# Two transformer blocks in fp32 on one core: gate logits in column groups, far rows, squares, expert order and fillers moved

## What is computed

```python
m = (silu_c @ ada_w[i] + ada_b[i])[:, None, :]            # adaptive vectors, sh1, sc1, g1, sh2, sc2, g2
o = dense_attention(q_rot, q, k, v, kc, vc)               # MLA heads, latent rows
y = o.reshape(B, S, H * DV) @ w_o                         # output projection
h_lat = layer_norm(DEEPNORM_ALPHA * h_lat + g1 * y, ln1_g[i], ln1_b[i])
f = conv_ffn(modulate(h_lat, sh2, sc2), ...)              # u = conv(h @ w_in); (silu(g) * a) @ w_out

# second block
gates = jax.nn.sigmoid(gate_logits.astype(f32)).reshape(b, s, G, R, 3)     # 24 columns of h @ w_in
o_hg = hgrn2_mixer(hg_q, hg_f, hg_i, lb)
o_hg = rmsnorm(o_hg, hg_norm[layer]) * jax.nn.silu(hg_g...)
for e in range(N_EXPERTS):                                # 32, d_ff 512
    hid = jax.nn.silu(t @ w_gate[e]) * (t @ w_up[e])
    out = out + combine[:, e:e + 1] * (hid @ w_down[e])
return rmsnorm(x, final_norm)
```

## Time and profile before

| | before |
|---|---|
| median of 3 runs | 1923.35 us (1923.25 to 1924.73) |
| the profiled execution | 1930.62 us, span 1928.9 us |
| mean granted PE clock | 0.966 |
| PE busy | 1761.5 us, 91% |
| weight loads of PE | 1363.9 us, 71% |
| DVE busy | 893.9 us, 46% |
| ACT busy | 362.7 us, 19% |
| DMA | 395.64 MB, 205 GB/s mean |

### The profile page before, as it was taken

How to read it: one execution, slowest core, us unless ns; L and a number is a source line. 1 busy time by engine, 2 the same in 40 slices (tenths; PEclk the granted TensorE clock), 3 DMA queues, 4 the chain that set the end, 5 groups by cost and what they waited for, 6 DMA issues and landing times.

```text
span 1928.9 us, 33169 instructions
## 1 busy us (share of the span) xinstructions
PE 1761.5 (91%) x14152; PEld 1363.9 (71%) x14152; DVE 893.9 (46%) x1909; ACT 362.7 (19%) x859; POOL 0.2 (0%) x4
## 2 busy tenths in 40 slices
PE   7999999999999999999999999999999766666666
PEld 4455546888888887777888888888788554555545
DVE  1488837766667327667554412478333211111112
ACT  0343403111110014222211102202321100000001
POOL 0000000000000000000000000000000000000000
PEclk9999999999999999999999999999999987888889
DMA  9534321222221207445344543323286999999996
GB/s 377 223 132 165 142 87 44 88 87 87 87 103 65 116 33 229 153 154 196 120 146 159 206 165 131 131 74 124 88 351 252 421 429 429 428 428 428 429 428 267
DMA packets 32508, 395.64 MB, mean 205 GB/s; under 512 B 3616, under 2 KB 6688, under 8 KB 8736
## 3 DMA queue, kind: packets, MB, share of 16 engines
q1 hardware_dynamic: 32416, 394.31, 51.2%
HBM read 393.25 MB, written 1.05 MB: 204 GB/s over the span
## 4 chain that ended last, share of the span: by engine, by line
PE 77%; DMA 19%; DVE 2%; ACT 1%; issue 1%; SPq 0%; DVEq 0%
PE bank L547 23%; DMA ring<-w_moe 17%; PE bank L1759 13%; PE bank L600 8%; PE bank L1487 6%; PE bank L3211 3%; PE bank L1972 3%; PE bank L843 2%; PE bank L1968 1%; PE bank L753 1%; PE bank L1145 1%; DMA ring<-w_ada 1%; PE bank L2328 1%; PE bank L1121 1%; PE bank L2024 1%
## 5 line engine op out<-in xcount | busy, mean ns | idle before, releaser
L547 PE MATMUL bank<-layer_input,ring 128*128 128x256 f32 x1152 | 257.4, 384 | 0.0
L547 PEld LDWEIGHTS bank<-layer_input,ring 128*128 128x128 f32 x1152 | 220.5, 193 | 33.1 <-issue 3.0
L3211 PE MATMUL bank<-ring,arena 128*32 128x128 f32 x1920 | 77.3, 326 | 54.6 <-DMA ring<-w_moe 52.1
L3328 DVE TENSOR_TENSOR arena<-arena,bank 128x128 f32<-128x128 f32 x32 | 9.2, 288 | 230.6 <-PE bank L3211 230.6
L1759 PE MATMUL bank<-arena 128*128 128x256 f32 x504 | 115.6, 379 | 0.0
L3211 PEld LDWEIGHTS bank<-ring,arena 128*32 128x32 f32 x1920 | 66.3, 131 | 66.5 <-DMA ring<-w_moe 61.8
L1487 PE MATMUL bank<-arena,ring 128*128 128x256 f32 x480 | 107.0, 380 | 2.4 <-ACT arena L1582 1.4
L1759 PEld LDWEIGHTS bank<-arena 128*128 128x128 f32 x504 | 95.8, 190 | 13.0
L1487 PEld LDWEIGHTS bank<-arena,ring 128*128 128x128 f32 x480 | 90.7, 190 | 16.5 <-ACT arena L1582 2.8
L600 PE MATMUL bank<-arena,ring 128*128 128x256 f32 x452 | 99.1, 380 | 0.9 <-DVE arena L2131 0.6
L3211 PE MATMUL bank<-arena 128*32 128x128 f32 x2008 | 70.2, 297 | 28.9 <-DMA arena<-w_moe 27.6
(11 more groups left out here) (484 smaller groups left out, 2708.7 us busy)
## 6 DMA issues: line engine op xcount, KB each, us to landing
arena<-w_moe SPq DMA_DIRECT2D x46, 2048.0 KB, 26.5
ring<-w_moe SPq DMA_DIRECT2D x45, 2048.0 KB, 25.9
ring<-w_ffn_in SPq DMA_DIRECT2D x22, 2048.0 KB, 8.0
ring<-w_ada_late SPq DMA_DIRECT2D x8, 3072.0 KB, 10.0
ring<-w_ffn_out SPq DMA_DIRECT2D x8, 2816.0 KB, 9.6
ring<-w_proj SPq DMA_DIRECT2D x7, 3072.0 KB, 10.2
ring<-w_na_pair SPq DMA_DIRECT2D x8, 1536.0 KB, 6.3
arena<-w_far SPq DMA_DIRECT2D x11, 1024.0 KB, 6.9
```

The costliest lines, as they stand in the source:

```text
L547: last = pe.matmul(out, a, b, start=(k == 0), stop=(k == len(lhs) - 1))
L3211: ins = eng.matmul(bank[x][group[q], 0:P], xe[:, k, SLOTS * e:SLOTS * e + SLOTS], weight(e, last, (x * KT + k) * FE + q * P, P), start=(k ...
```

## The change

Five things are moved. (1) In the last head pair, the adaptive chunk has five tiles (`ADA_LAST`, `ada_tiles`), which takes two products of rows from DVE; eight fillers stand ahead of the transposes and three behind the value product; DVE's first `mid` of every pair goes between the two rounds of maxima; the barrier at the end of the stage becomes two waits of PE. (2) In `out_split` the far rows' rest becomes a step of its own, `FAR_REST`, between products 6 and 7. (3) The gate logits are summed in four groups of 32 columns in `gate_sums`, DVE copies the groups, and two products with a constant (`fold24`) add them, behind the spread; three fillers instead of four. (4) ACT takes the recurrence's squares at head four. (5) The expert kept in spare memory is the third (2) instead of the 29th (28); the first quad is written out without a scatter and the two clears ahead of it go; in the last quad the scatter of experts 28 and 29 comes behind expert 30's gate, the held gate of expert 31 ahead of expert 30's down, experts 30 and 31 are scattered from tiles of their own in two turns of row groups (`scatter_alone`), and the last down matrix is loaded in two pieces.

```diff
@@ heads @@
+        if who == "pe":
+            b, taken, before = self.mla_turn(s, ("ada", ADA_LAST))
+            eng.wait_ge(taken, before + 1)
+            self.fill(eng, 3, b)
+            _, taken, before = self.mla_turn(s, ("av", MLA_PAIRS - 1))
+            eng.wait_ge(taken, before + 1)
         self.ada_rest(who, eng)
-        self.phase_end(eng, who)
...
-            half = 4 + u % 2
+            half = 6 if u == ADA_LAST else 4 + u % 2
...
             ada(u, 0)
+            if u == ADA_LAST:
+                b = claim(("av", u))
+                self.fill(pe, 8, b)
             turn(u)
...
             dve.tensor_scalar(nb[:, 0:4], mx[:, 0:4], -scale, None, ALU.mult).then_inc(s["max_ready"], 1)
+            mid(u, 0, 0)
             dve.wait_ge(s["scored"], 2 * u + 2)
...
-            mid(u, 0, 0)
             turned(u)
-            mid(u, 0, 1)
-            ada(u)
-            mid(u, 1, 0)
-            attended(u)
-            mid(u, 1, 1)
+            if u < ADA_LAST:
+                mid(u, 0, 1)
+                ada(u)
+                mid(u, 1, 0)
+                attended(u)
+                mid(u, 1, 1)
+            else:
+                ada(u)
+                mid(u, 0, 1)
+                attended(u)
@@ out_split @@
                 if i == 6:
                     eng.wait_ge(s["snapped"], OUT_SNAPPED[c, 4])
                     eng.wait_ge(s["sums_ready"], ready + (4 if c else 7))
+                    last = product(a, w21, t3, False)
+                if i == FAR_REST:
                     eng.wait_ge(s["up_used"], used_0 + c)
-                    rest(d, c, 1, CTX, start=True)
-                    last = product(a, w21, t3, False)
+                    last = rest(d, c, 1, CTX, start=True)
...
-                eng.wait_ge(s["up_done"], OUT_DONE[c, 6])
+                eng.wait_ge(s["up_done"], OUT_DONE[c, FAR_REST])
@@ mixer, PE @@
+            for k in range(KT):
+                j = 32 * (k % 4)
+                last = pe.matmul(bank[6][j:j + 32, 0:LAT], self.V[:, w + k * 24:w + k * 24 + 32], x[k], start=(k < 4),
+                                 stop=(k >= 4), skip_group_check=True)
+            last.then_inc(s["front_mm"], 1)
         def gate_logits():
+            pe.wait_ge(s["cmp_steps"], self.GATE_COPIED)
             for t in range(2):
-                last = self.mm(pe, bank[6][:, t * 24:(t + 1) * 24], [xk[:, t * P:(t + 1) * P] for xk in x],
-                               [self.vec("w_gate24", k * 24, 24) for k in range(KT)])
+                last = pe.matmul(bank[6][:, LAT + t * 24:LAT + (t + 1) * 24], sums[:, t * P:(t + 1) * P],
+                                 self.con("fold24"), start=True, stop=True)
             last.then_inc(s["front_mm"], 1)
...
         first_groups()
+        gate_sums()
+        spread()
         gate_logits()
-        spread()
-        self.fill(pe, 4)
+        self.fill(pe, 3)
@@ mixer, DVE @@
         dve.memset(v["blk"], 0.0).then_inc(s["cmp_steps"], 1)
+        dve.wait_ge(s["front_mm"], self.GATE_SUMS)
+        dve.tensor_copy(v["E0"][:, 0:LAT], bank[6][:, 0:LAT]).then_inc(s["cmp_steps"], 1)
@@ mixer, ACT @@
-            if u == 5:
+            if u == 4:
                 act.wait_ge(s["hg_mm"], self.HG_OUT)
@@ router @@
-        for n in ("gwt", "y"):
-            dve.memset(v[n], 0.0)
@@ experts @@
-RESIDENT = EXPERTS - QUAD
+RESIDENT = 2
...
+        sp.dma_start(self.expert_slots()[e][:, UPS:split], self.W["moe"][LAST][:, UPS:split])\
+            .then_inc(self.expert_loaded()[e][2], 16)
+        sp.dma_start(self.expert_slots()[e][:, split:], self.W["moe"][LAST][:, split:]).then_inc(self.sem("kept_in"), 16)
...
+        def scatter_alone(e, turn):
+            for t in range(2):
+                for h in ((turn + t) % 2, (turn + t) % 2 + 2):
+                    q = group[(h + e) % 4]
+                    ins = eng.matmul(bank[4 + 2 * t + h // 2][:, (h % 2) * 256:(h % 2) * 256 + 256], gwt[q, h, t, :],
+                                     alone[e][q, :], start=False, stop=(e == QUAD - 1), skip_group_check=True)
+                    if e == 2 or not turn:
+                        ins.then_inc(link, 1)
...
-                    if e == 0:
+                    if e == 0 and not first:
...
+                    if last and e == 2:
+                        eng.wait_ge(s["gwt_copied"], i * 2 + 2)
+                        eng.wait_ge(s["y_dve"], x + 1)
+                        eng.wait_ge(s["y_act"], x + 1)
+                        for t in range(2):
+                            scatter(t)
...
+                    if last and e == 2:
+                        eng.wait_ge(s["silu_done"], x + 1)
+                        project(0, QUAD - 1, last=True).then_inc(s["gate_done"], 1)
...
+                    if e == QUAD - 1 and last:
...
+                        scatter_alone(2, 0)
+                        eng.wait_ge(link, quads + 4)
+                        scatter_alone(2, 1)
...
-            with eng.Fori(0, quads - 1) as i:
+            quad(0, first=True)
+            with eng.Fori(1, quads - 1) as i:
                 quad(i)
-            quad(quads - 1, True)
+            quad(quads - 1, last=True)
             eng.wait_ge(s["y_dve"], EXPERTS + 1)
-            eng.wait_ge(s["y_act"], EXPERTS + 1)
-            for t in range(2):
-                scatter(t, stop=True).then_inc(self.sem("var_ready"), 1)
+            eng.wait_ge(link, quads + 8)
+            scatter_alone(3, 0)
+            eng.wait_ge(link, quads + 12)
+            scatter_alone(3, 1)
```

149 lines of the change are left out of this document (96 added, 53 removed).

## The result

The changed kernel takes 1911.36 us (median of 4 executions, 1909.52 to 1912.92) beside 1923.82 for the kernel before (4 executions); the ratio is 0.9934, 95% interval 0.9917 to 0.9952. That is 12.5 us, where 18.6 was forecast: it is faster, as forecast, but 6.7 us above the predicted time (1904.7) and 0.4 above the range. Over the whole study the changed kernel was taken three times (13 executions, median 1909.95) beside 72 executions of the kernel before on three chips (median 1924.94, 1922.8 to 1929.2), with ratios of 0.9934, 0.9921 (0.9904 to 0.9937) and 0.9922 (0.9908 to 0.9935). So the change is worth some 12.5 to 15 us; the median of all 13 lies inside the range, 5.2 us above the forecast.

The account below looks back on a forecast made before the run. Bound: TensorE until about 1490 us, then the experts' weight stream at 428 GB/s. Terms 4.3 + 1.9 + 2.4 + 5.0 + 5.0 = 18.6 us took the median to 1904.7; range 1899.5 to 1911.0.

Parts of the forecast that it names:

- The base: Differences read from the profiled execution, 1930.62 us, carried unscaled to the unprofiled median, 1923.35, which is 7.3 less.
- Squares: Recurrence, squares moved to head four: 1.6 us wait before head five's sum goes, and 3.4 of half speed; 5.0 us.
- Heads' end: Last head pair: output projection starts at about 241.8 instead of 244.40, 2.6 us, plus 1.7 of clock; 4.3 us.
- Transposes and the clock: Last head pair: 2.8 us of transposes might count as a gap for the clock, losing the 1.7 us.
- Far rows: First feed-forward's second product: 0.64 us wait on ScalarE goes in three of four output chunks; 1.9 us, between 1.0 and 2.0.
- Gate logits: Projection after the gates 2.0 us sooner, up to 1.9 more by the clock; 2.4 us taken, between 0 and 4.0.
- Experts: Expert stage: start, end and closing scatter, (a) to (c), with rounding for one stall; 5.0 us, between -1 and 8.
- (a): Start of the expert stage: without the first scatter, 3.72 us, the hole in the weight stream shrinks; 0.7 us.
- (b): End of the expert stage: PE keeps up with the stream, last weights land at 1909.6, last product ends at 1913.2.
- (c): Closing scatter in two turns: 1.5 us in all against 3.72, first half summed at 1914.9 against ScalarE's start at 1919.66.
- The first, the clock: Rival: the clock falls anyway in thin stretches left; 1.7 + 3.4 + 0.9 us lost, giving 1910.7; chance 0.13.
- the second rival: Experts' gain does not come: PE at 0.50 in last quad, scatter before expert 30's up; 5.0 lost, 1909.7; chance 0.18.

## Why the prediction was wrong

- **The base.** "I carry the sum of differences over to it unscaled" is the step that failed. The profiled execution stood 7.3 us above the median, and I named the number and asked no further. A second execution took 1923.98, and the excess lay in the very places that I priced: 3.3 us at head five, 1.6 at the gate logits, 1.8 in the experts. What an unusual execution loses can't be won back from the usual one. The term that it spoiled most is the next.
- **Squares, 5.0.** Mis-sized: 1.9 us (1.7 in the traces of usual executions). The wait of 1.6 was right. The half speed that I priced at 3.4 came in 2 of 6 executions, 3.3 us each time, and both were the slowest of their kernels; by that frequency it is worth about 1.1 in the mean and nothing in the median.
- **Heads' end, 4.3.** Right: 3.8 to 4.6 alone, 4.5 in the traces. The steps stand too: the projection at 241.5 (forecast 241.8), DVE's product out of the way, 1.7 us of clock (in the four of seven executions without the edit in which the projection's clock fell). Of the value product's start I had 238.2, and it was 237.87.
- **Transposes and the clock.** In the changed kernel 24 transposes behind fillers ran in 3.21 us at 1.00, and the projection began at 1.00; without the fillers they took 4.53 with the clock at 0.50, and the projection still began at 1.00. By the rule of the Trainium skill ("TensorE: Matmul & The Clock Gate", Part 4, PE-mode transpose) the 1.7 us would have stayed lost; in ten executions with this edit, nine of them with fillers, they never were.
- **Far rows, 1.9.** The traces show 2.2, the times 0.6 to 0.9 with an interval that holds both. The mechanism is seen, its size is not settled by the times.
- **Gate logits, 2.4.** Right in size: 1.5 to 1.7 alone, 2 to 4 within the whole. From the last product of the norm's sums to the sixtieth record of the projection the traces read 21.6 us in the mean of eight executions without the edit and 18.7 in nine with it. The new wait for the copy (forecast 0.6, measured 0.98) was foreseen. A fall of the clock and "the clock at 1.00" both occurred, in 3 and 6 of 9 executions.
- **Experts, 5.0.** Mis-sized: 3.9 in the traces, 2.5 to 2.9 alone by the times. (a) gives nothing: the hole in the stream stays, so the first scatter was not its cause, and the second one, which did go, brings the end of the stream no nearer. (b) and (c) together were to give 4.3 and gave 3.9, of which up to 2 may be the stall inside expert 31's up, which no step of the sum named. The closing scatter, from last down to the end, gave 1.3 (14.2 to 12.9), less than my step (c), since ScalarE had read the first half while PE was summing the second in the old kernel too. Two turns of one scatter take 1.6 us with their wait, as the row of the rope scores gave (1.5). But "here only two work together" was a misreading. Within a turn the four products use four different row groups, and 30 ns behind the first start four records are in work at once:

```profile
1897.32:1897.34 0.02, 0.02 (x4) 0.02 (x4) 0.00 (x0) 0.00 (x0) 0.00 (x0) 1.00 0.00 0
```

  The 3.07 times that the Trainium skill gives for four row groups ("TensorE: Matmul & The Clock Gate", Part 3, Measured speedup) would make it 1.2, by an estimate from that figure; here 3.72 against 1.6 is 2.3 times, with two turns and the 0.17 us of wait between them.
- **The rivals.** The first, the clock, came in another form than I gave it: not that falls stay in the changed kernel, but that they were not in the usual kernel before. (At the gate logits they do stay, in 3 of 9.) I had made it 1910.7 at a chance of 0.13; that this is close to what was measured is luck, since the terms that make it up are others. Half-speed work at expert 30's gate, part of the second rival, is real: 3.5 to 3.6 us instead of 1.95 in three of six executions with this end, and the stage 1.6 us longer in them. The stream did not starve.

With the terms at their measured sizes, 4.5 + 2.2 + 2.7 + 1.7 + 3.9 and 0.7 for the weights of the second product, the sum is 15.7. From the median of the 72 executions of before, 1924.94, that gives 1909.2, and 13 executions of the changed kernel gave 1909.95. The 12.5 of the first comparison is a small sample on both sides: before had 1923.82 there, the changed kernel 1911.36. So of the 6.1 us between 18.6 and 12.5, 2.9 are terms (squares 3.3 and experts 1.1 too large, the others together 1.5 too small), 2.5 are that sample (15.0 over all executions), and 0.7 stay unexplained.

## What to carry to other kernels

Before a half-speed stretch is priced from a trace, look whether that execution is a usual one: if its time stands several us above the median, the excess is in the trace, and most likely in the places one is about to repair. In this kernel a clock fall behind a short wait came in some executions and not in others, so price it with that frequency, and the wait itself in full. Ask of half-speed work whether PE would have waited at its end anyway: expert 29's down cost nothing at half speed, expert 30's gate 1.6 us. At the end of a stream-bound stage, order on PE is worth only what lies between PE's chain and the last landing; measure that distance first (here it was under 2 us after the change).

## What the hardware showed that I had not expected

- The same wait of 1.59 us ahead of the same work was followed by a fall to 0.50 in two executions and not in four. Nothing in the rows around it tells them apart, and what decides it stays open.
- A gap of 2.51 us at the heads' end was followed by transposes at the upper level in five of seven executions, one of 0.43 plus 0.98 us at the gate logits by a fall in three of nine.
- The edit at the heads' end also removed a wait for the feed-forward's output weights near 590 us: it is 0.45 to 1.13 us in all eight executions without the edit or its fillers, 0.19 in one of the nine with both, and absent in the other eight. By what link was not tried.
- The first four executions of the changed kernel lie at 1909.5, 1909.9, 1912.8 and 1912.9. The profiles of this kernel were all taken at 1908.9 to 1910.8, so what makes the upper pair is open.
